# Layer normalisation's root in halves of 256 tokens, an output pair that ends one by one, and four moved or added pieces of work, in a three-layer forward pass

## The chip, the cores and the metric

One core of a Trainium2 chip runs the whole kernel. The metric is the device time in microseconds (us) of one execution; the times given are medians of three. TensorE multiplies matrices into the eight banks of PSUM (128 x 512 float32 each). VectorE, ScalarE and GpSimd (POOL in the rows) compute tile by tile, and SyncE (SP) issues the transfers that bring weights from memory. The engines run independently and wait for each other at semaphores.

## What is computed

512 tokens of width 1024, batch 1, float32. First block, two layers:

```python
for i in range(2):
    m = _even_mixer(x, ...) if i % 2 == 0 else _odd_mixer(x, ...)
    x = _layer_norm(DN_ALPHA * x + m, ln1_g[i], ln1_b[i])
    x = _layer_norm(DN_ALPHA * x + _sq_relu_mlp(x, w_up[i], w_down[i]), ln2_g[i], ln2_b[i])
    gate = jax.nn.sigmoid(x @ ple_w_gate[i] + ple_b_gate[i])
    x = x + gate * (p[i] @ ple_w_proj[i])

def _layer_norm(x, g, b):
    mu = jnp.mean(xf, -1, keepdims=True)
    var = jnp.mean(jnp.square(xf - mu), -1, keepdims=True)
    y = (xf - mu) * lax.rsqrt(var + NORM_EPS)
    return (y * g + b)
```

The even mixer joins a latent attention (queries and keys from small root-mean-square-normalised latents; each head's key is 64 own rows and a rotated part that all eight heads share) and a sliding-window attention. The odd mixer is a causal attention of 16 heads with forget gates. The hidden width of the squared-relu MLP is 4096. The second block, one layer, works on `x` after that: root-mean-square norm, four branches of 256 channels (a gated linear recurrence, pooling over time, an indexed sparse attention, attention to 256 memory vectors), a gate for each, an output projection with a norm behind it, and a gated feed-forward network of hidden width 2816.

## The kernel before

**Tiles.** Activations lie transposed: 128 channels on the partitions, 512 tokens along a row, so `X` and `ACC` have eight tiles of 128x512. Float32 products are made of three products of rounded operands: a weight tile `RAW` (up to 128x1024) is rounded to `WH` by ScalarE (`hi_ahead`, L354 to L364), and its remainder `WL` (the "low part") is made by VectorE (`lo_ahead`, `lo_one`, L366 to L380), or at some places by GpSimd (also through `lo_one`, L370), both three tiles ahead of their use, in four slots. Activations have `XH` (rounded) and `XL` (remainder). A linear output is then WH·XH, WH·XL and WL·XH over the eight tiles (L400 to L402), accumulated in one of the PSUM banks 0 and 1 in turn; an engine evacuates the bank before it is used again. Each engine's order is written out by hand, piece by piece, with the same walk over the weight tiles (`st`) on all of them.

**Layer normalisation** (four times: `ln1_0`, `ln2_0`, `ln1_1`, `ln2_1`). TensorE sums over the channels with matrices of ones (`ln_pe`, L682): the mean lies in bank 7, the mean square in bank 6. Then:
- ScalarE (`ln_act`, L745): the negative mean `MEAN`, its square, and, once VectorE has the variance, Ln and Exp (the first guess `RS` of the root) and the Square of it into bank 7 (`PB[7]`). Then the weight tile due, and the rounding of the eight tiles into `XH` (L764).
- VectorE (`ln_dve`, L788): the centred tile 0 (L791), variance (L793), floor and epsilon (L795), then one Newton step in two links (L798 in place in bank 7, L800 into bank 6), then for each tile the scale by gain and root (L806) and, one tile later, the remainder `XL` (L810). All links are 128x512.
- GpSimd (`ln_pool`, L766): the sums for mean and mean square over tiles 1 to 6 (L776, L781), then the mean added to tiles 1 to 7 of `ACC` (L783), and behind the last `XL` the sums `X = ACC + bias` of all eight tiles (L786), which the next residual uses (in the MLP, VectorE waits for all of them ahead of the first residual; in the gates, VectorE waits for tile `o` ahead of its step on output `o`).

**The pair behind each normalisation** (`lin_pair`, L1276). The first two linear outputs after it are begun together in banks 0 and 1, so that each new `XH` tile feeds four products and each `XL` tile two. Both end with the same last tile; their last two products stand directly behind each other. The third output then needs bank 0 evacuated.

**MLP** (`mlp` on each engine). Loops of four outputs: TensorE's 24 products each; VectorE makes the next low part, then the relu into `HR` (L2550), then the remainder `HL` (L2552); ScalarE rounds the weight tile three ahead, squares (L1982) and rounds (L1984). Then the down products, 16 weight tiles for 8 outputs.

**Gates of the first block** (`ple`). For each output: Tanh on ScalarE, two steps on VectorE (`GP`, then the new `X`), in layer 1 then a Square of `X` on ScalarE (L1999) that GpSimd sums up (L1143), and in between the memory vectors are transposed (L1262) and split (`ML`, L2586).

**Latent attention, keys.** VectorE rotates the shared part `KR`; GpSimd copies it below each of the eight heads' keys (`KM[64:128, h]`). VectorE writes the head's own part from each `ukv` output (L2455), behind the low part that it owes (`step()` makes the low part, then waits for the output).

**End of the recurrent branch and last gates.** GpSimd makes the low parts of nine gate weight tiles (`N_GATE[0] + 3` and on), `G_LAST[5]` among them. VectorE makes the branch's root (L712) and its output's remainder `YBL`/`y_lo` (L2961), which TensorE's gate products L1375 follow.

**Four outputs begun together** (`lin_quad`, L1549). The first four feed-forward outputs wait for the first rounded tile of the normalised input (`XH`, L2238); VectorE afterwards makes the norm's root `RU` (L3041) and the first product `TG` (L3054), which frees the first of four banks.

Of the kernel before, what the change touches and what calls it, by code (L numbers as in the profile page):

```python
# [95 lines left out]
def program(nc, known, t):  # L96
# [3 lines left out]
    with ctx:  # L100
# [358 lines left out]
        def pe_scores(pe, kind, g, qb):  # L459
# [15 lines left out]
            if kind == "mla" and qb == 0:  # L475
                evac_of(pe, M_A["uq", 2 * g])
                evac_of(pe, M_A["uq", 2 * g + 1])
                evac_of(pe, M_A["ukv", 2 * g])
                evac_of(pe, M_A["ukv", 2 * g + 1])
                pe.wait_ge(sem["chain_p"], cnt.value("chain_p", "krope"))  # L480
# [263 lines left out]

        def ln_act(act, key, b, st=None):  # L745
# [5 lines left out]
            act.wait_ge(sem["ln_v"], cnt.value("ln_v", key))  # L751
            done(act.activation(RS[:], TMP[:], ACT.Ln), "rs_ln", key)
            act.wait_ge(sem["rs_ln"], cnt.value("rs_ln", key))
            done(act.activation(RS[:], RS[:], ACT.Exp, scale=-0.5), "chain_a", ("rs", key))
            act.wait_ge(sem["chain_a"], cnt.value("chain_a", ("rs", key)))
            done(act.activation(PB[7][:], RS[:], ACT.Square), "rs_exp", key)
# [5 lines left out]
            for j in range(DT):  # L762
                act.wait_ge(sem["norm"], cnt.value("norm", (key, j)))
                done(act.activation(XH[:, j], ACC[:, j], ACT.Identity, bias=VEC[:, b + j:b + j + 1]), "x_hi", (key, j))  # L764

        def ln_pool(pool, key, b):  # L766
# [17 lines left out]
            pool.wait_ge(sem["x_lo"], cnt.value("x_lo", (key, DT - 1)))  # L784
            for j in range(DT):
                done(pool.tensor_scalar(X[:, j], ACC[:, j], VEC[:, b + j:b + j + 1], None, ALU.add), "x_full", (key, j))  # L786

        def ln_dve(dve, key, g, b):  # L788
# [4 lines left out]
            done(dve.scalar_tensor_tensor(TMP[:], PB[6][:], 1.0 / D, MEANSQ[key[:3]], ALU.mult, ALU.subtract), "chain_d", ("v", key))  # L793
            dve.wait_ge(sem["chain_d"], cnt.value("chain_d", ("v", key)))
            done(dve.tensor_scalar(TMP[:], TMP[:], 0.0, 1e-5, ALU.max, ALU.add), "ln_v", key)  # L795
            dve.wait_ge(sem["ln_v"], cnt.value("ln_v", key))
            dve.wait_ge(sem["rs_exp"], cnt.value("rs_exp", key))
            done(dve.scalar_tensor_tensor(PB[7][:], PB[7][:], -0.5, TMP[:], ALU.mult, ALU.mult), "chain_d", ("n2", key))  # L798
            dve.wait_ge(sem["chain_d"], cnt.value("chain_d", ("n2", key)))
            done(dve.scalar_tensor_tensor(PB[6][:], PB[7][:], 1.5, RS[:], ALU.add, ALU.mult), "misc_free", ("mean", key))  # L800
            dve.wait_ge(sem["misc_free"], cnt.value("misc_free", ("mean", key)))
            for j in range(DT + 1):
                if j < DT:
                    if j:
                        dve.wait_ge(sem["cen"], cnt.value("cen", (key, j)))
# [315 lines left out]
        def _(pool):  # L1121
# [7 lines left out]
            pool.wait_ge(sem["kr"], cnt.value("kr", "twice"))  # L1129
            for h in range(8):  # L1130
                x = pool.tensor_copy(KM[64:128, h], KR[64:128, :])
            done(x, "chain_p", "krope")
            pool.wait_ge(sem["chain_p"], cnt.value("chain_p", "krope"))
# [36 lines left out]
            for n in range(N_GATE[0] + 3, N_GATE[0] + 12):  # L1170
                lo_one(pool, n)
# [18 lines left out]
        def _(pe):  # L1190
# [85 lines left out]
            def lin_pair(rh, rl, names, key):  # L1276
# [7 lines left out]
                for k in range(DT + 1):  # L1284
                    if k < DT:
                        wait(pe, names[0], (key, k))
                        for e in range(2):
                            s = slots[e][0]
                            pe.matmul(PB[ms[e] % 2][:], WH[:, s, k], rh[:, k], start=k == 0, stop=False)  # L1289
                            pe.matmul(PB[ms[e] % 2][:], WL[:, s, k], rh[:, k], start=False, stop=False)  # L1290
                    if k:
                        wait(pe, names[1], (key, k - 1))
                        for e in range(2):
                            s = slots[e][0]
                            x = pe.matmul(PB[ms[e] % 2][:], WH[:, s, k - 1], rl[:, k - 1], start=False, stop=k == DT)  # L1295
                            if k == DT:
                                x.then_inc(used[s], 1)
# [3 lines left out]
            def second_pe():  # L1301
# [247 lines left out]
                def lin_quad(rh, rl, names, key):  # L1549

                    slots = [st.slot(e) for e in range(4)]
                    for o in (6, 7):
                        pe.wait_ge(sem["brf"], cnt.value("brf", o))

# [310 lines left out]
        def _(act):  # L1865
# [101 lines left out]

            def mlp(l):
                pa = st.n - 1
                for half in range(2):  # L1970
# [16 lines left out]
                    if half == 0:  # L1987
                        split_loop(16, 8)

            def ple(l):  # L1990
# [9 lines left out]
                for what in PLE_TILES:  # L2000
                    hi_ahead(act, st)
                    if isinstance(what, int):
# [4 lines left out]
                        act.activation(GT[:, what % 2], PB[b][:], ACT.Tanh, bias=HB[:, l * 8 + what:l * 8 + what + 1], scale=0.5).then_inc(evac[b], 1)  # L2007
                        st.m += 1
# [351 lines left out]
        def _(dve):  # L2360
# [55 lines left out]
            def event(what, i):  # L2416
# [778 lines left out]
```

## Time and profile before

| | us |
|---|---|
| time, median of 3 | 2248.16 (2247.05 to 2248.75) |
| the profiled execution, its own time | 2248.09 |
| its span | 2246.3 |
| TensorE busy, products | 2182.3 (97%) |
| VectorE busy | 1263.6 (56%) |
| ScalarE busy | 884.7 (39%) |
| GpSimd busy | 303.8 (14%) |

The profile is of one execution. A row of the timeline is start, duration, engine, line, operation, output and inputs with their shapes, and in brackets the idle time of the engine before it with what ended it. A row of the waits is engine, output and line of the waiting instruction, `<-` and who released it, then the total in us, the number of times and the longest. "PE" is TensorE, "DVE" VectorE, "ACT" ScalarE. Rows of an execution add up to the span, which leaves out the 1.8 us around it.

### The profile page before, as it was taken

How to read it: one execution, taken by the hardware profiler on the slowest of the kernel's cores; microseconds unless marked ns; L12 is line 12 of the kernel's file. 1: busy time of each engine (PE TensorE's matmuls, PEld its weight loads, DVE VectorE, ACT ScalarE, POOL GpSimd, SP SyncE). 2: the span in 40 equal slices, each digit the busy share in tenths (PEclk: the TensorE clock that was granted, in tenths of full speed). 3: DMA queues.
4: the chain of work that ended last, by engine and by line, in shares of the span. 5: the costliest groups of instructions: out<-in, count | busy, mean ns of one | idle time of the engine just before them, and what ended most of it. 6: DMA issues, size and time to landing. Idle time of an engine off the chain costs nothing.

```text
span 2246.3 us, 27968 instructions
## 1 busy us (share of the span) xinstructions
PE 2182.3 (97%) x10176; PEld 1725.5 (77%) x10176; DVE 1263.6 (56%) x1992; ACT 884.7 (39%) x1462; POOL 303.8 (14%) x192
## 2 busy tenths in 40 slices
PE   7999999999999999999999999999999999999998
PEld 5767788888777777788888777678778787888886
DVE  5676643343474554643343477388589678544554
ACT  3555442233254445442243254433543444222333
POOL 0000700001330001600001450133000330000001
PEclk9999999999999999999999999999999999999999
DMA  6112233333224331333333234123222232323322
GB/s 173 27 49 92 76 102 103 94 93 103 75 77 110 87 95 49 93 103 103 94 93 103 85 95 109 49 79 110 74 67 66 67 112 74 99 81 112 94 68 73
DMA packets 368307, 196.92 MB, mean 88 GB/s; under 512 B 21040, under 2 KB 362813, under 8 KB 368206
## 3 DMA queue, kind: packets, MB, share of 16 engines
q1 hardware_dynamic: 367794, 195.51, 30.4%
q8 instruction: 63, 1.03, 0.2%
q14 instruction: 38, 0.31, 0.0%
q10 hardware_dynamic: 412, 0.07, 0.0%
HBM read 193.40 MB, written 2.14 MB: 87 GB/s over the span
## 4 chain that ended last, share of the span: by engine, by line
PE 84%; DVE 9%; issue 3%; ACT 2%; POOL 1%; ACTq 0%; DVEq 0%; POOLq 0%
PE PB L400 22%; PE PB L402 21%; PE PB L401 21%; PE PB L483 2%; PE PB L529 2%; PE PB L1389 2%; PE PB L1391 2%; PE PB L1390 2%; PE PB L502 2%; DVE ATT L2925 1%; DVE WL L370 1%; POOL X L786 1%; PE PB L1289 1%; PE PB L1290 1%; PE PB L1295 1%
## 5 line engine op out<-in xcount | busy, mean ns | idle before, releaser
L364 ACT ACTIVATE WH<-RAW 128x1024 fp32r<-128x1024 f32 (+3 forms) x365 | 369.1, 1015 | 374.4 <-PE PB L402 353.4
L400 PE MATMUL PB<-XH,WH 128*128 128x512 f32 x1232 | 487.7, 396 | 6.6 <-DVE HR L2550 1.9
L402 PE MATMUL PB<-XH,WL 128*128 128x512 f32 x1232 | 480.9, 390 | 0.0
L401 PE MATMUL PB<-XL,WH 128*128 128x512 f32 x1232 | 480.0, 390 | 0.0
L380 DVE TENSOR_TENSOR WL<-RAW,WH 128x1024 fp32r<-128x1024 f32 x184 | 237.4, 1290 | 172.6 <-ACT WH L364 162.2
L400 PEld LDWEIGHTS PB<-XH,WH 128*128 128x128 f32 x1232 | 231.3, 188 | 60.7 <-issue 3.3
L402 PEld LDWEIGHTS PB<-XH,WL 128*128 128x128 f32 x1232 | 231.1, 188 | 49.5
L401 PEld LDWEIGHTS PB<-XL,WH 128*128 128x128 f32 x1232 | 231.5, 188 | 47.6 <-issue 0.7
L370 DVE TENSOR_TENSOR WL<-RAW,WH 128x1024 fp32r<-128x1024 f32 (+2 forms) x156 | 188.1, 1212 | 61.2 <-ACT WH L364 60.6
L400 PE MATMUL PB<-HH,WH 128*128 128x512 f32 x512 | 199.2, 389 | 0.0
L401 PE MATMUL PB<-HL,WH 128*128 128x512 f32 x512 | 199.2, 389 | 0.0
L402 PE MATMUL PB<-HH,WL 128*128 128x512 f32 x512 | 199.2, 389 | 0.0
L776 POOL TENSOR_TENSOR SM<-ACC 128x512 f32<-128x512 f32 x4 | 5.2, 1294 | 870.6 <-DVE ACC L2535 523.1
L1982 ACT ACTIVATE HS<-HR 128x512 f32<-128x512 f32 x64 | 40.5, 632 | 193.2 <-DVE HR L2550 193.2
L616 ACT ACTIVATE PT<-PB 128x256 f32<-128x256 f32 (+3 forms) x160 | 65.5, 412 | 124.5 <-PE PB L502 124.4
L402 PEld LDWEIGHTS PB<-HH,WL 128*128 128x128 f32 x512 | 96.1, 188 | 20.1
L400 PEld LDWEIGHTS PB<-HH,WH 128*128 128x128 f32 x512 | 96.1, 188 | 20.0
L401 PEld LDWEIGHTS PB<-HL,WH 128*128 128x128 f32 x512 | 96.1, 188 | 19.8
L2552 DVE TENSOR_TENSOR HL<-HS,HH 128x512 f32 x64 | 44.3, 692 | 107.0 <-ACT HH L1984 107.0
L370 POOL TENSOR_TENSOR WL<-RAW,WH 128x1024 fp32r<-128x1024 f32 (+1 forms) x33 | 69.0, 2103 | 260.8 <-ACT WH L364 138.4
L1389 PE MATMUL PB<-XH,WH 128*128 128x512 f32 x256 | 102.9, 402 | 0.4 <-ACT RS L2090 0.4
L1391 PE MATMUL PB<-XH,WL 128*128 128x512 f32 x256 | 99.8, 390 | 0.0
(518 smaller groups left out, 3648.3 us busy)
## 6 DMA issues: line engine op xcount, KB each, us to landing
RAW<-in_w_up SPq DMA_DIRECT2D x64, 512.0 KB, 3.9
RAW<-in_w_down SPq DMA_DIRECT2D x64, 512.0 KB, 3.6
RAW<-in_w_ffn_gate_up SPq DMA_DIRECT2D x44, 512.0 KB, 3.7
RAW<-in_w_gate SPq DMA_DIRECT2D x32, 512.0 KB, 4.0
RAW<-in_od_w_in SPq DMA_DIRECT2D x24, 512.0 KB, 6.2
RAW<-in_w_in SPq DMA_DIRECT2D x24, 512.0 KB, 4.0
RAW<-in_ple_w_gate SPq DMA_DIRECT2D x16, 512.0 KB, 3.7
RAW<-in_w_ffn_down SPq DMA_DIRECT2D x16, 512.0 KB, 4.0
```

Source lines behind the costliest of these rows:

```text
L364: act.activation(WH[:, s, 0:nb], RAW[:, s, 0:nb], ACT.Copy).then_inc(hi_done[s], 1)
L370: eng.tensor_tensor(WL[:, s, 0:nb], RAW[:, s, 0:nb], WH[:, s, 0:nb].bitcast(F32), ALU.subtract).then_inc(lo_done[s], 1)
L380: dve.tensor_tensor(WL[:, s], RAW[:, s], WH[:, s].bitcast(F32), ALU.subtract).then_inc(lo_done[s], 1)
L400: pe.matmul(PB[b][0:m, 0:n], WH[:, s, k, 0:m], rh[:, kk, :], start=kk == 0, stop=False)
L401: pe.matmul(PB[b][0:m, 0:n], WH[:, s, k, 0:m], rl[:, kk, :], start=False, stop=False)
L402: x = pe.matmul(PB[b][0:m, 0:n], WL[:, s, k, 0:m], rh[:, kk, :], start=False, stop=kk == last)
L483: xs[e] = pe.matmul(PB[2 + e][:, lo:lo + w], q[:, qb * P:qb * P + P], k[:, ks[0] * P:ks[0] * P + w], start=True, stop=plain)
L502: x = pe.transpose(PB[4 + e][:, c * P:c * P + P], PR[:, e, c * P:c * P + P], ID[:])
L529: x = pe.matmul(PB[6][e * 64:e * 64 + 64, q0 * P:q1 * P], vs[e](j), PT[:, e, j, q0 * P:q1 * P], start=first, stop=lastp)
L616: done(act.activation(PT[:, e, ks[0]:ks[0] + len(ks), qb * P:qb * P + P], PB[4 + e][:, 0:len(ks) * P].rearrange("p (j q) -> p j q", q=P), ...
L1389: pe.matmul(PB[m % 2][:], WH[:, n % 4, k], XH[:, k], start=k == 0, stop=False)
L1391: x = pe.matmul(PB[m % 2][:], WL[:, n % 4, k], XH[:, k], start=False, stop=k == DT - 1)
```

## The change

1. **Root in halves.** Variance, floor, Ln, Exp, Square, both Newton links, and scale and rounding of tile 0 are made for tokens 0 to 255 and then for 256 to 511. Variance and floor of both halves come first on VectorE; then, for each half, the Newton links and the scale. The Square no longer writes PSUM bank 7 but `VT`, a tile in SBUF, and the first Newton link works in place there. The weight tile of ScalarE stays behind both Squares.
2. **The pair ends one by one.** With the last tile the first output gets its products ahead of the second's: it ends two products ahead of it, not one.
3. **Sums by ScalarE.** The eight L786 leave GpSimd. After `ln1` ScalarE makes them between the up and the down products of the MLP's first half, after `ln2` one behind each Tanh of the gates.
4. **Key copies by ScalarE** in the slots of the first three `uq` events (3, 3, 2), and around them VectorE makes the low part after each pair of `KM` products, two at a time.
5. **Low part of `G_LAST[5]`** from GpSimd to VectorE, behind `y_lo`.
6. **Relu first** in the MLP loops: `lo_ahead` stands behind the relu, not ahead of the wait for the output.
7. **Warm products.** Ahead of the four outputs begun together TensorE makes 13 products of 512 columns whose result is overwritten.

```diff
-                pe.wait_ge(sem["chain_p"], cnt.value("chain_p", "krope"))
+                pe.wait_ge(sem["chain_a"], cnt.value("chain_a", "krope"))
...
+        TOKEN_HALVES = (slice(0, T // 2), slice(T // 2, T))
...
-            done(act.activation(RS[:], TMP[:], ACT.Ln), "rs_ln", key)
-            act.wait_ge(sem["rs_ln"], cnt.value("rs_ln", key))
-            done(act.activation(RS[:], RS[:], ACT.Exp, scale=-0.5), "chain_a", ("rs", key))
-            act.wait_ge(sem["chain_a"], cnt.value("chain_a", ("rs", key)))
-            done(act.activation(PB[7][:], RS[:], ACT.Square), "rs_exp", key)
+            for c, part in enumerate(TOKEN_HALVES):
+                act.wait_ge(sem["ln_v"], cnt.value("ln_v", (key, c)))
+                done(act.activation(RS[:, part], TMP[:, part], ACT.Ln), "rs_ln", (key, c))
+                act.wait_ge(sem["rs_ln"], cnt.value("rs_ln", (key, c)))
+                done(act.activation(RS[:, part], RS[:, part], ACT.Exp, scale=-0.5), "chain_a", ("rs", key, c))
+                act.wait_ge(sem["chain_a"], cnt.value("chain_a", ("rs", key, c)))
+                done(act.activation(VT[:, part], RS[:, part], ACT.Square), "rs_exp", (key, c))
...
-            for j in range(DT):
+            for c, part in enumerate(TOKEN_HALVES):
+                act.wait_ge(sem["norm"], cnt.value("norm", (key, "first") if c == 0 else (key, 0)))
+                x = act.activation(XH[:, 0, part], ACC[:, 0, part], ACT.Identity, bias=VEC[:, b:b + 1])
+            done(x, "x_hi", (key, 0))
+            for j in range(1, DT):
...
-            pool.wait_ge(sem["x_lo"], cnt.value("x_lo", (key, DT - 1)))
-            for j in range(DT):
-                done(pool.tensor_scalar(X[:, j], ACC[:, j], VEC[:, b + j:b + j + 1], None, ALU.add), "x_full", (key, j))
...
+            for c, part in enumerate(TOKEN_HALVES):
+                done(dve.scalar_tensor_tensor(TMP[:, part], PB[6][:, part], 1.0 / D, MEANSQ[key[:3]][:, part], ALU.mult, ALU.subtract), "chain_d", ("v", key, c))
+                dve.wait_ge(sem["chain_d"], cnt.value("chain_d", ("v", key, c)))
+                done(dve.tensor_scalar(TMP[:, part], TMP[:, part], 0.0, 1e-5, ALU.max, ALU.add), "ln_v", (key, c))
+            for c, part in enumerate(TOKEN_HALVES):
+                dve.wait_ge(sem["ln_v"], cnt.value("ln_v", (key, c)))
+                dve.wait_ge(sem["rs_exp"], cnt.value("rs_exp", (key, c)))
+                done(dve.scalar_tensor_tensor(VT[:, part], VT[:, part], -0.5, TMP[:, part], ALU.mult, ALU.mult), "chain_d", ("n2", key, c))
+                dve.wait_ge(sem["chain_d"], cnt.value("chain_d", ("n2", key, c)))
+                root = dve.scalar_tensor_tensor(PB[6][:, part], VT[:, part], 1.5, RS[:, part], ALU.add, ALU.mult)
...
+                done(dve.scalar_tensor_tensor(ACC[:, 0, part], ACC[:, 0, part], VEC[:, g:g + 1], PB[6][:, part], ALU.mult, ALU.mult), "norm", (key, "first") if c == 0 else (key, 0))
...
-            pool.wait_ge(sem["kr"], cnt.value("kr", "twice"))
-            for h in range(8):
-                x = pool.tensor_copy(KM[64:128, h], KR[64:128, :])
-            done(x, "chain_p", "krope")
-            pool.wait_ge(sem["chain_p"], cnt.value("chain_p", "krope"))
...
             for n in range(N_GATE[0] + 3, N_GATE[0] + 12):
-                lo_one(pool, n)
+                if n != G_LAST[5]:
+                    lo_one(pool, n)
...
+                wait(pe, names[0], (key, DT - 1))
+                wait(pe, names[1], (key, DT - 2))
+                rounded(0, DT - 1)
+                low(0, DT - 2)
+                rounded(1, DT - 1)
+                wait(pe, names[1], (key, DT - 1))
+                low(0, DT - 1).then_inc(used[slots[0][0]], 1)
+                low(1, DT - 2)
+                low(1, DT - 1).then_inc(used[slots[1][0]], 1)
...
+                    pe.wait_ge(lo_done[slots[0][0]], slots[0][1] + 1)
+                    for _ in range(13):
+                        pe.matmul(PB[2][:], WH[:, slots[0][0], 0], WH[:, slots[0][0], 0:4], start=True, stop=True)
...
+                    if what == "uq" and i < 3:
+                        act.wait_ge(sem["kr"], cnt.value("kr", "twice"))
+                        for h in range(3 * i, min(3 * i + 3, 8)):
+                            x = act.activation(KM[64:128, h], KR[64:128, :], ACT.Copy)
+                        if i == 2:
+                            done(x, "chain_a", "krope")
...
+            def x_full(key, j):
+                b = VCOL[key[:3] + "_b", int(key[-1])]
+                done(act.activation(X[:, j], ACC[:, j], ACT.Identity, bias=VEC[:, b + j:b + j + 1]), "x_full", (key, j))
...
                     if half == 0:
+                        for j in range(DT):
+                            x_full(f"ln1_{l}", j)
                         split_loop(16, 8)
...
+                        x_full(f"ln2_{l}", what)
...
-                    step()
+                    lin_ready(dve, st)
                     dve.tensor_tensor(KM[0:64, i], PB[b][0:64], RK[0:64, :], ALU.mult).then_inc(evac[b], 1)
+                    if i % 2:
+                        lo_one(dve, st.n + 2)
+                        lo_one(dve, st.n + 3)
...
-                            lo_ahead(dve, st, k, i, 4)
                             lin_ready(dve, st, k, i, 4)
                             b, ub = st.bank(k, i, 4)
                             dve.tensor_scalar(HR[:, k % 2], PB[b][:], 0.0, None, ALU.max).then_inc(evac[b], 1)
+                            lo_ahead(dve, st, k, i, 4)
...
+                lo_one(dve, G_LAST[5])
```

## Rows read from the trace of the kernel before

**Rows 1.** The page: the span, and the busy time of each engine.

```profile
span 2246.3 us, 27968 instructions
...
PE 2182.3 (97%) x10176; PEld 1725.5 (77%) x10176; DVE 1263.6 (56%) x1992; ACT 884.7 (39%) x1462; POOL 303.8 (14%) x192
```

**Rows 2.** Waits of TensorE by line and releaser: us in all, times, longest.

```profile
PE PB L1289 <- ACT XH L764: 8.0, 7, 1.9
...
PE PB L1262 <- DVE ML L2586: 3.9, 2, 3.5
...
PE PB L1556 <- ACT XH L2238: 3.5, 1, 3.5
...
PE PB L483 <- DVE KM L2455: 2.8, 1, 2.8
...
PE PB L400 <- DVE HR L2550: 1.9, 2, 1.4
```

**Rows 3.** Timeline of the second normalisation (start, us, engine, line).

```profile
608.07 1.05 DVE L795 TENSOR_SCALAR TMP<-TMP 128x512 f32<-128x512 f32 x1
...
608.79 1.48 POOL L783 TENSOR_TENSOR ACC<-ACC,SM 128x512 f32<-128x512 f32 x1
...
611.92 0.70 DVE L800 SCALAR_TENSOR_TENSOR PB<-PB,RS 128x512 f32<-128x512 f32 x1
...
613.96 1.28 POOL L783 TENSOR_TENSOR ACC<-ACC,SM 128x512 f32<-128x512 f32 x1
...
614.26 1.52 DVE L810 SCALAR_TENSOR_TENSOR XL<-ACC,VEC,XH 128x512 fp32r<-128x512 f32 x1 [0.20 <-ACT XH L764]
...
614.31 0.47 PE L1289 MATMUL PB<-XH,WH 128*128 128x512 f32 x1 [1.52 <-ACT XH L764]
```

**Rows 4.** Single lines: ns of one (least, median, most), from and to.

```profile
L810 DVE SCALAR_TENSOR_TENSOR XL<-ACC,VEC,XH x32: 737/740/1533, 252.7 to 1298.6; 128x512 fp32r<-128x512 f32 x32
...
L2668 DVE SCALAR_TENSOR_TENSOR MRB<-MRB,MRB x1: 425/425/425, 1346.7 to 1346.7; 128x256 f32<-128x256 f32 x1
...
L2774 DVE TENSOR_TENSOR SC<-SC,CHK x3: 294/1265/2386, 1476.8 to 1480.5; 128x128 f32<-128x128 f32 x3
```

**Rows 5.** Timeline: small additions beside GpSimd's low parts.

```profile
1476.62 2.40 POOL L370 TENSOR_TENSOR WL<-RAW,WH 128x1024 fp32r<-128x1024 f32 x1 [6.34 <-ACT WH L364]
...
1476.77 2.39 DVE L2774 TENSOR_TENSOR SC<-SC,CHK 128x128 f32<-128x128 f32 x1
...
1479.19 1.26 DVE L2774 TENSOR_TENSOR SC<-SC,CHK 128x128 f32<-128x128 f32 x1
```

**Rows 6.** Windows, TensorE: us, busy (products), granted clock, DMA share, GB/s.

```profile
350.00:400.00 50.00, 50.00 (x222) 1.00 0.32 95
...
1864.60:1867.90 3.30, 3.30 (x9) 0.50 0.46 136
```

**Rows 7.** Timeline of the gates of layer 1.

```profile
1316.33 1.55 POOL L1143 TENSOR_TENSOR SM<-SQR 128x512 f32<-128x512 f32 x1
...
1317.97 0.63 ACT L1999 ACTIVATE SQR<-X 128x512 f32<-128x512 f32 x1 [3.12 <-POOL SM L1143]
...
1320.87 0.30 PE L1262 MATMUL PB<-ID,MIN 128*128 128x128 f32 x1 [3.55 <-DVE ML L2586]
```

**Rows 8.** Timeline at the end of the recurrent branch.

```profile
1778.16 2.70 DVE L712 SCALAR_TENSOR_TENSOR HGB<-HGB,HGB 128x512 f32<-128x512 f32 x1
...
1783.06 0.47 PE L1375 MATMUL PB<-YBH,WH 128*128 128x512 f32 x1 [1.46 <-DVE YBL L2961]
```

**Rows 9.** Timeline behind the four outputs begun together.

```profile
1882.50 0.69 DVE L3041 SCALAR_TENSOR_TENSOR RU<-VT,RS 128x512 f32<-128x512 f32 x1
...
1883.29 0.69 DVE L3054 TENSOR_TENSOR TG<-PB,RU 128x512 f32<-128x512 f32 x1
...
1899.39 0.50 PE L400 MATMUL PB<-XH,WH 128*128 128x512 f32 x1 [0.56 <-DVE TG L3054]
```

**Rows 10.** Timeline before the first keys of the latent attention.

```profile
128.60 0.41 DVE L370 TENSOR_TENSOR WL<-RAW,WH 128x256 fp32r<-128x256 f32 x1
```

More of the change, by code:

```diff
@@ L750, in ln_act @@
             done(act.activation(MEANSQ[key[:3]], MEAN, ACT.Square), "m2", key)
-            act.wait_ge(sem["ln_v"], cnt.value("ln_v", key))
-            done(act.activation(RS[:], TMP[:], ACT.Ln), "rs_ln", key)
-            act.wait_ge(sem["rs_ln"], cnt.value("rs_ln", key))
-            done(act.activation(RS[:], RS[:], ACT.Exp, scale=-0.5), "chain_a", ("rs", key))
-            act.wait_ge(sem["chain_a"], cnt.value("chain_a", ("rs", key)))
-            done(act.activation(PB[7][:], RS[:], ACT.Square), "rs_exp", key)
+            for c, part in enumerate(TOKEN_HALVES):
[5 more added lines that the diff above has]
+                done(act.activation(VT[:, part], RS[:, part], ACT.Square), "rs_exp", (key, c))
             if key[:3] == "ln2":
@@ L792, in ln_dve @@
             dve.wait_ge(sem["m2"], cnt.value("m2", key))
[L793 to L798, printed above, removed]
@@ L799, in ln_dve @@
-            dve.wait_ge(sem["chain_d"], cnt.value("chain_d", ("n2", key)))
-            done(dve.scalar_tensor_tensor(PB[6][:], PB[7][:], 1.5, RS[:], ALU.add, ALU.mult), "misc_free", ("mean", key))
-            dve.wait_ge(sem["misc_free"], cnt.value("misc_free", ("mean", key)))
+            for c, part in enumerate(TOKEN_HALVES):
+                done(dve.scalar_tensor_tensor(TMP[:, part], PB[6][:, part], 1.0 / D, MEANSQ[key[:3]][:, part], ALU.mult, ALU.subtract), "chain_d", ("v", key, c))
+                dve.wait_ge(sem["chain_d"], cnt.value("chain_d", ("v", key, c)))
+                done(dve.tensor_scalar(TMP[:, part], TMP[:, part], 0.0, 1e-5, ALU.max, ALU.add), "ln_v", (key, c))
@@ new lines, in ln_dve @@
+            for c, part in enumerate(TOKEN_HALVES):
[4 more added lines that the diff above has]
+                root = dve.scalar_tensor_tensor(PB[6][:, part], VT[:, part], 1.5, RS[:, part], ALU.add, ALU.mult)
+                if c == 0:
+                    done(root, "rsq", (key, "first"))
+                    dve.wait_ge(sem["rsq"], cnt.value("rsq", (key, "first")))
+                else:
+                    done(root, "misc_free", ("mean", key))
+                    dve.wait_ge(sem["misc_free"], cnt.value("misc_free", ("mean", key)))
+                done(dve.scalar_tensor_tensor(ACC[:, 0, part], ACC[:, 0, part], VEC[:, g:g + 1], PB[6][:, part], ALU.mult, ALU.mult), "norm", (key, "first") if c == 0 else (key, 0))
@@ L802, in ln_dve @@
             for j in range(DT + 1):
-                if j < DT:
-                    if j:
-                        dve.wait_ge(sem["cen"], cnt.value("cen", (key, j)))
+                if 0 < j < DT:
+                    dve.wait_ge(sem["cen"], cnt.value("cen", (key, j)))
                     done(dve.scalar_tensor_tensor(ACC[:, j], ACC[:, j], VEC[:, g + j:g + j + 1], PB[6][:], ALU.mult, ALU.mult), "norm", (key, j))
@@ L1283, in lin_pair, with rounded, low @@
                     pe.wait_ge(lo_done[slots[e][0]], slots[e][1] + 1)
[L1284 to L1290, printed above, removed]
+                def rounded(e, k):
+                    s = slots[e][0]
+                    pe.matmul(PB[ms[e] % 2][:], WH[:, s, k], rh[:, k], start=k == 0, stop=False)
+                    pe.matmul(PB[ms[e] % 2][:], WL[:, s, k], rh[:, k], start=False, stop=False)
+                def low(e, k):
+                    return pe.matmul(PB[ms[e] % 2][:], WH[:, slots[e][0], k], rl[:, k], start=False, stop=k == DT - 1)
+                for k in range(DT - 1):
+                    wait(pe, names[0], (key, k))
+                    for e in range(2):
+                        rounded(e, k)
                     if k:
@@ L1293, in lin_pair @@
                         for e in range(2):
[L1294 to L1297, printed above, removed]
+                            low(e, k - 1)
+                wait(pe, names[0], (key, DT - 1))
[7 more added lines that the diff above has]
+                low(1, DT - 1).then_inc(used[slots[1][0]], 1)
                 st.n += 2
```

## The prediction

> **What bounds the kernel now.** I read the page first: TensorE is busy for 2182 of 2246.3 us [rows 1]. So a microsecond is won or lost only where TensorE waits, or where its products run at the lower clock. The list of TensorE's waits comes next [rows 2]. Its longest line is the one this change aims at: the first products after each of the four layer normalisations wait for the first rounded tile XH, 8.0 us in 7 waits (four of 1.5 to 1.9, three of about 0.4). The products wait once 3.5 us in the middle of the gates of layer 1, and once 3.5 us ahead of the four outputs begun together. Third, I read the second normalisation on all engines [rows 3], to see which link is late and beside what it runs. Last, the windows give the clock: in a stretch of full work 222 products take 50 us, 0.225 each; right after the 3.5 us wait the clock reads 0.50 (1.2 GHz) and 9 products take 3.3 us [rows 6]. The trace has four such falls of some 3.4 us, each costing up to 1.7 us.
>
> **The normalisation in halves.** The chain is variance, floor (L795), Ln, Exp, Square, two Newton steps (L798, L800), scale (L806), round (L764). Cutting a 128x512 link into two of 256 columns should let the two halves overlap on two engines. A half link on VectorE takes 0.43 us [rows 4]. One on ScalarE lies between 0.32 and 0.63, half and all of a full one [rows 7]; I take 0.42.
>
> But the Square no longer goes to bank 7 of PSUM. It goes to VT, in SBUF, so both Newton steps now read two SBUF tiles (VT and TMP, VT and RS), and they run while GpSimd adds the mean to seven tiles back to back (L783). The rows say what that costs. L800 reads one PSUM tile (before, its first input lies in bank 7) and one SBUF tile beside those additions and takes 0.70 [rows 3], as all eight such steps do. L810 reads two SBUF tiles: 0.74 alone, but 1.52 when it starts inside an addition [rows 3, 4], and it ends 0.55 after GpSimd's. L795 (SBUF to SBUF) is held up too, 1.05 [rows 3], against about 0.43 for the part left when GpSimd's addition ends. The closest case is two dependent additions of 128x128 behind two queued GpSimd instructions: 0.29 alone, 2.39 the first, 1.26 the second [rows 4, 5]. The second asked 0.03 us after the first had ended and still had to let GpSimd's next instruction through: 1.0 us of waiting for every such step.
>
> The Trainium skill has this as a rule (page SBUF — State Buffer, section Who interferes with whom): VectorE and GpSimd share one pair of SBUF ports, a VectorE instruction with two SBUF inputs takes it exclusively against a GpSimd one that reads SBUF, and the later one blocks until the first is through. By this rule the halves below queue up; the trace agrees (1.52 against 0.74).
>
> Worked through for the second normalisation. The first floor half ends at 608.98 (L795's end less half its work). The second floor half: 1.0 + 0.29, 610.27. First half of Newton step one: 1.0 + 0.43, 611.70 (ScalarE's three halves are over by 610.3, at worst 610.9, inside that wait). Step two 613.13, step one of the second half 614.56, step two 615.99. Scale half 0.47, round half 0.51, and the latencies of today: TensorE starts at 617.15 instead of 614.31 [rows 3], 2.8 later. All seven additions of GpSimd are used up just then. From there TensorE is fed as fast as it works (1.32 us for a tile on VectorE, six products of 0.225 on TensorE), the short wait of 0.4 goes, and L810 of tile 0 no longer stands behind GpSimd. Left: +2.4. Three times 2.4 and 1.9 for the third one, whose floor asks just as an addition ends (1.3 or 2.4): **+9.1**. Bounds from both sides: -1.3 each if no step is held up, +2.9 each if nothing is won back.
>
> The wait ahead of these products grows from 1.5 to 1.9 us to about 4.3. Waits of 3.5, 3.5 and 2.8 us [rows 2] had a fall of the clock behind them, and so had the first normalisation with 1.9; the three others, with 1.5 to 1.8, had none. At 4.3 I expect it behind all four, 1.7 us each for the three new ones: **+5.1**, bounds 0 and +7.5 (a fall of twice the length).
>
> **Outputs begun together.** Output 0 of the pair ended one product (0.225 us) ahead of output 1 and now ends two ahead, while output 1 ends as before: its evacuation starts 0.23 earlier. That counts at five places, where the third output waits for it: behind the four normalisations (0.4 to 1.4 us, two of them in [rows 2]) and behind the pair at 1822. In the third one a low part (1.2 us) stands ahead of the relu, which begins 0.6 after its bank is full; with the relu moved ahead of it that goes too. 5 x 0.23 + 0.6 = 1.75: **-1.7**, bounds 0 and -2.7. In the MLP loops the low part is still two tiles ahead of its use, so its later place costs nothing; the cover is some 9 us of products.
>
> **Sums by ScalarE.** GpSimd's eight L786 go. In the MLP, ScalarE does them (8 x 0.6 = 5 us) between the up and down products, and VectorE waits for them there; the first residual is needed two tiles, 11 us, later: nothing, with 5 us of cover left. In the gates each stands behind the Tanh: 0.6 us more before VectorE's two steps. At the end of layer 0 this uses 0.5 of 1.1 us of slack. In layer 1 the 3.5 us wait is in truth GpSimd's: it is late with its eight sums, so its first sum of squares starts at 1316.33, ScalarE's square waits for that until 1317.97, and the transposes until 1320.87 [rows 7]. With GpSimd free, that square follows the Tanh and x_full at about 1316.0. Then VectorE's X step queues behind one GpSimd addition, and the transposes come at 1319.4, of which 0.6 is already in an earlier wait. -1.5 us, and with a wait of 1.5 instead of 3.5 no fall of the clock: -1.7. Together **-3.2**, bounds +0.6 and -5.
>
> **One low part from GpSimd to VectorE.** L712 takes 2.70 us instead of 0.69 because GpSimd makes the low part of gate 5 beside it, and TensorE waits 1.46 us at its end [rows 8]. Moved behind y_lo it ends 1.5 us before its product: **-1.4**, bounds 0 and -1.5.
>
> **Key copies.** GpSimd's eight were hidden. On ScalarE the last five (2.5 us) delay a high part by 1.6 and with it VectorE by 0.3. Against that two low parts of 0.41 us, 0.33 each from start to start [rows 10], move behind the two KM products that TensorE waits for (2.8 us): **-0.4**, bounds +0.5 and -0.7.
>
> **Warm products.** 13 x 0.225 = 2.9 us fit into the 3.5 us wait ahead of the four outputs [rows 2] and keep the clock up: 1.3 us earlier for TensorE. But what is late next is VectorE. RU is finished at 1883.19 and TG starts at 1883.29 [rows 9]; from there VectorE and ScalarE run link after link until the TG that TensorE waits 0.56 us for at 1899.39. That wait grows by what was won: **-0.1**, bounds -0.1 and +1.7 (a fall of the clock behind the longer wait).
>
> **Sum.** 9.1 + 5.1 - 1.7 - 3.2 - 1.4 - 0.4 - 0.1 = +7.4. The profiled execution took 2248.09 us (span 2246.3 [rows 1]), the median is 2248.16, so they stand for each other: 2255.5 us.
>
> **Rivals.** (a) *The split works as meant.* If GpSimd lets the halves through, or they fall between its additions, each normalisation starts 1.3 us earlier and none drops the clock: -5.2 - 1.7 - 3.2 - 1.4 - 0.4 - 0.1 = -12.0, 2236 us, faster. For it: the halves are short and 0.1 us lies between two additions. Against: no two-SBUF step that starts inside a two-input GpSimd instruction gets through fast, among more than 40. It decides as soon as two of the six held steps per chain find the port free. (b) *The halves queue, but the clock holds*, or falls once: 5.1 or 3.4 less than the forecast, 2250.4 to 2252.1, no change. For it: a wait of 2.3 us at 1745 had no fall. Against: all three waits over 2.5 us had one. (c) *The falls last twice as long*, or ScalarE's added sums come late in the gates and the 3.5 us wait stays (3.2): 2259 to 2261. Against: the falls in the trace are all single.
>
> **How the numbers follow.** Forecast 0.56 (2252 to 2259, by the smaller terms' bounds; a seventh of it under +0.2%), (a) 0.17, (b) 0.17, (c) 0.10. A difference of about 0.2% (4.5 us) is what a measurement of this kernel can tell from none. Faster 0.17; same 0.17 + 0.08 = 0.25; slower 0.48 + 0.10 = 0.58. The range leaves (a) out and takes in the others with the bounds of the smaller terms (-3 at the lower end of (b), and (c) whole): 2246 to 2261.
>
> **What would show it.** Right: both halves of Newton steps one and two at 1.0 to 1.4 us instead of 0.43 beside L783; TensorE's wait for XH at 3.9 to 4.5 us, four times; windows behind it with the clock at 0.50; the transposes in the gates waiting 1 to 2 us; no wait at y_lo; a wait of about 1.8 us for TG. Wrong: Newton halves at 0.43 and a wait for XH under 1 us.

## The result and the profile after

The changed kernel takes 2259.34 us (2257.77 to 2260.14) against 2248.18; the ratio is 1.0049, 95% interval 1.0037 to 1.0061: slower by half a percent. The forecast was 2255.5, range 2246 to 2261, slower with 0.58. The profiled execution took 2257.77 us, the lowest of six, so the traces account for +9.7 us, and 1.6 us of the median stand in other executions. In all that follows one execution is left out, of the kernel with the key copies alone: it took 2444.86 us at a granted clock of 0.912.

The page of the changed kernel, its busy times (to be read against [rows 1]):

```profile
span 2255.6 us, 28037 instructions
...
PE 2187.8 (97%) x10187; PEld 1731.7 (77%) x10189; DVE 1270.4 (56%) x2013; ACT 912.3 (40%) x1518; POOL 232.6 (10%) x151
```

GpSimd has 71 us less to do, ScalarE 28 more, and neither matters: TensorE's waits do. The list of these, after (for [rows 2]: line and releaser, us in all, times, longest):

```profile
PE PB L1293 <- ACT XH L767: 17.8, 4, 4.6
...
PE PB L1269 <- DVE ML L2622: 3.3, 2, 1.7
...
PE PB L483 <- DVE KM L2488: 2.2, 1, 2.2
...
PE PB L400 <- DVE TG L3091: 1.3, 1, 1.3
...
PE PB L1576 <- ACT XH L2271: 0.6, 2, 0.3
```

The wait that the halves should shorten went from 8.0 us in seven waits to 17.8 in four. Those at ML, KM and ahead of the four outputs are shorter, the one at TG longer. Why XH is late stands in the timeline of the second normalisation (for [rows 3]; start, us, engine, line, operation, tiles, and in brackets the idle time before with its releaser; x7 are seven instructions joined):

```profile
606.17 9.38 POOL L790 TENSOR_TENSOR ACC<-ACC,SM 128x512 f32<-128x512 f32 x7 [9.17 <-ACT SM L750]
...
607.67 1.18 DVE L800 TENSOR_SCALAR TMP<-TMP 128x256 f32<-128x256 f32 x1
...
609.22 0.94 DVE L800 TENSOR_SCALAR TMP<-TMP 128x256 f32<-128x256 f32 x1
...
610.32 1.28 DVE L804 SCALAR_TENSOR_TENSOR VT<-VT,TMP 128x256 f32<-128x256 f32 x1
...
611.63 1.41 DVE L806 SCALAR_TENSOR_TENSOR PB<-VT,RS 128x256 f32<-128x256 f32 x1
613.08 0.48 DVE L813 SCALAR_TENSOR_TENSOR ACC<-ACC,VEC,PB 128x256 f32<-128x256 f32 x1
613.47 0.96 DVE L804 SCALAR_TENSOR_TENSOR VT<-VT,TMP 128x256 f32<-128x256 f32 x1
...
614.47 1.37 DVE L806 SCALAR_TENSOR_TENSOR PB<-VT,RS 128x256 f32<-128x256 f32 x1
...
617.05 0.77 PE L1293 MATMUL PB<-XH,WH 128*128 128x512 f32 x1 [4.39 <-ACT XH L767]
```

Six links of 256 columns take 0.94 to 1.41 us, while L813, as wide but with a PSUM input, takes 0.48 among them. A link that was 0.70 at full width [rows 3] takes 1.41 at half. The windows of TensorE (us, busy with products in brackets, granted clock, DMA share, GB/s) show what followed the wait, for [rows 6]:

```profile
350.00:400.00 50.00, 50.00 (x223) 1.00 0.36 105
617.00:621.50 4.50, 4.45 (x11) 0.50 0.02 5
...
615.50:622.20 6.70, 5.15 (x12) 0.50 0.01 4
622.40:626.00 3.60, 3.60 (x18) 1.00 0.00 0
253.70:257.00 3.30, 3.30 (x9) 0.50 0.00 0
...
1755.60:1757.40 1.80, 1.77 (x8) 0.50 0.00 0
```

In the second normalisation the clock is at 0.50 from 615.5 on, while TensorE still waits, and until 622.3, 6.8 us in all. Twelve products in it take 5.15 us, against 2.7 at 0.225 each: 2.4 us are lost, at three of the four normalisations. The first has a fall of 3.4 us, as it had before.

Laid side by side, product by product, the two timelines give where the changed kernel falls behind (+) or catches up, worked out from the start of the same product in both (us; the rows add up to +9.4, which is, but for rounding, what the two spans differ by):

| stretch | forecast | measured |
|---|---|---|
| key copies and the clock behind KM | -0.4 | -2.5 |
| start behind the four normalisations | +2.8, +2.8, +2.3, +2.8 | +2.5, +2.9, +2.9, +2.9 |
| from there to the third output: slow products, short waits gone, the pair, the relu | +2.0 | +3.6 |
| gates of layer 1 | -3.2 | -2.5 |
| fall of the clock behind the 2.3 us wait in the recurrent branch | 0 | +1.6 |
| low part of gate 5 | -1.4 | -1.6 |
| pair at 1822, warm products up to TG | -0.3 | -0.4 |

### The profile page after: what moved, and what is told of

It is laid out like the page before. It is cut to its first block, busy times and chain, and to the rows that moved or that the text cites. A ratio compares the mean times of both kernels' runs of the same rounds, so it can differ in the third digit from the quotient of the medians.

```text
span 2255.6 us, 28037 instructions
## 1 busy us (share of the span) xinstructions
PE 2187.8 (97%) x10187; PEld 1731.7 (77%) x10189; DVE 1270.4 (56%) x2013; ACT 912.3 (40%) x1518; POOL 232.6 (10%) x151
## 4 chain that ended last, share of the span: by engine, by line
PE 85%; DVE 9%; issue 3%; ACT 2%; DMA 0%; POOL 0%; DVEq 0%; SPq 0%; ACTq 0%; POOLq 0%
PE PB L400 21%; PE PB L402 21%; PE PB L401 21%; PE PB L483 2%; PE PB L1406 2%; PE PB L1408 2%; PE PB L1407 2%; PE PB L529 2%; PE PB L502 2%; PE PB L1293 1%; PE PB L1294 1%; DVE ATT L2961 1%; PE PB L1297 1%; DVE WL L370 1%; DVE PB L806 0%
## 5 line engine op out<-in xcount | busy, mean ns | idle before, releaser
L401 PE MATMUL PB<-XL,WH 128*128 128x512 f32 x1232 | 479.5, 389 | 0.0
L2585 DVE TENSOR_SCALAR HR<-PB 128x512 f32<-128x512 f32 x64 | 44.3, 692 | 147.9 <-PE PB L402 143.7
L1407 PE MATMUL PB<-XL,WH 128*128 128x512 f32 x256 | 99.7, 390 | 0.0
```

The source lines that it names most:

```text
L401: pe.matmul(PB[b][0:m, 0:n], WH[:, s, k, 0:m], rl[:, kk, :], start=False, stop=False)
L1407: pe.matmul(PB[m % 2][:], WH[:, n % 4, k], XL[:, k], start=False, stop=False)
```

## Experiments

**Where the loss sits.** Two kernels divide the change. In one the normalisation's functions on ScalarE and VectorE are the old ones, all else is changed:

```diff
-            for c, part in enumerate(TOKEN_HALVES):
-                act.wait_ge(sem["ln_v"], cnt.value("ln_v", (key, c)))
...
-                done(act.activation(VT[:, part], RS[:, part], ACT.Square), "rs_exp", (key, c))
...
+            done(act.activation(RS[:], TMP[:], ACT.Ln), "rs_ln", key)
...
+            done(act.activation(PB[7][:], RS[:], ACT.Square), "rs_exp", key)
```

> The changed kernel with the normalisation as before: full width, Square in bank 7; the sums X + bias stay on ScalarE, and the other parts of the change stay. The traces put +11.1 us of later starts and +4.6 us of slower products behind them on the halves; without them 2259.3 - 15 = 2244 us, 4 under the kernel before, 1.6 either way with the fall of the clock behind the wait of 2.3 us in the recurrent branch. If the other parts cost as much as they bring, 2248.

2240.79 us, ratio 0.997 (0.9957 to 0.9982): faster than before. The other has the halves alone, on the kernel before.

> The kernel before with the normalisation's halves alone, GpSimd's sums X + bias still behind them. If the halves carry the loss, 2248.2 + 15 = 2263 us, or a little more since the pair's and the relu's gains are missing: slower than the whole change. If the loss needs another part of the change too, under 2259.

2263.67 us, ratio 1.0065 (1.0048 to 1.0081). So the halves cost 15.3 us alone, by the runs of the kernel before made beside it (2248.35), and 18.5 within the change. Everything else together brings 7.6 us without them and 4.3 with them. The first kernel came out 3 us under what was expected; its trace has neither the fall of the clock behind the first normalisation (wait 1.87 us) nor that in the recurrent branch (2.25 us). It has one at a place where no other trace has it, behind two idle times of 0.7 us:

```profile
680.80:684.10 3.30, 3.30 (x13) 0.50 0.02 7
```

Its six executions, at 2239.5 to 2243.7, have granted clocks of 0.998 down to 0.995. That fits a fall behind a wait near 2 us in some executions and not in others, but only one of the six has a trace.

**Width or place of the operands.** Full width again, but the Square still in VT (the conditions that ask for the first part follow and are left out here):

```diff
-        TOKEN_HALVES = (slice(0, T // 2), slice(T // 2, T))
+        TOKEN_HALVES = (slice(0, T),)
```

> The changed kernel with the root at full width again (one part of 512 tokens), but the Square still in VT, so that both Newton links still have two inputs in SBUF. The old normalisation at full width, with bank 7, gave 2240.8 us. If the place of the operands costs and not the width, two links per normalisation are held by GpSimd (0.6 to 0.7 us over their 0.69 each), TensorE's wait for XH is 2.3 to 3 us, and the slow products behind it stay: about 2249 us. If VT is harmless, 2241.

2248.86 us, ratio 1.0005 (0.9996 to 1.0014), 8 us over the same width with bank 7, and a wait of 3.0 us on average. Its waits, and its second Newton link (ns: least, median, most):

```profile
PE PB L1293 <- ACT XH L767: 12.1, 4, 3.9
```

```profile
L806 DVE SCALAR_TENSOR_TENSOR PB<-VT,RS x4: 1641/1655/1660, 250.6 to 1290.5; 128x512 f32<-128x512 f32 x4
```

1.65 us where the same step with a PSUM input took 0.70 [rows 3]. The place of the Square alone is worth 8 of the 18.5 us. The other 10.5 come with the halving, which makes twice as many links, each of them held.

The smallest undoing: the first Newton link writes bank 7, so that only the second link has a PSUM input.

```diff
-                done(dve.scalar_tensor_tensor(VT[:, part], VT[:, part], -0.5, TMP[:, part], ...
+                done(dve.scalar_tensor_tensor(PB[7][:, part], VT[:, part], -0.5, TMP[:, part], ...
-                root = dve.scalar_tensor_tensor(PB[6][:, part], VT[:, part], 1.5, RS[:, part], ...
+                root = dve.scalar_tensor_tensor(PB[6][:, part], PB[7][:, part], 1.5, RS[:, part], ...
```

> The changed kernel, where each half's first Newton link reads VT and TMP as before but writes PSUM bank 7, so that the second reads PSUM and one SBUF tile. By the port: the two root halves (L806, 1.37 to 1.41 us) fall to 0.43, the two first Newton halves stay at 0.9 to 1.3; TensorE's wait for XH falls from 4.4 to 2.3 to 2.9 us; 1.5 to 2.1 us four times, with the falls of the clock still there: about 2252 us. If halving costs by itself, nothing changes: 2258 to 2260.

2245.29 us, ratio 0.9987 (0.9978 to 0.9997), 14 us gone with one operand (11 between the two profiled executions). More than expected: TensorE's wait came to 2.05 us (second normalisation), the falls behind it are 8 products instead of 12, and the first Newton link of the second half asked at a better moment (0.53 us instead of 0.96). The second link in the changed kernel, and then both links here:

```profile
L806 DVE SCALAR_TENSOR_TENSOR PB<-VT,RS x8: 1373/1388/1414, 247.3 to 1297.1; 128x256 f32<-128x256 f32 x8
```

```profile
L804 DVE SCALAR_TENSOR_TENSOR PB<-VT,TMP x8: 533/918/1295, 248.2 to 1288.5; 128x256 f32<-128x256 f32 x8
L806 DVE SCALAR_TENSOR_TENSOR PB<-PB,RS x8: 432/432/433, 249.5 to 1289.1; 128x256 f32<-128x256 f32 x8
```

The first link writes PSUM here and is held all the same, up to 1.30 us: what counts is where a link reads.

**Is GpSimd the holder?** Same VectorE code as in the change, but GpSimd's additions begin only when the root is done:

```diff
+            pool.wait_ge(sem["misc_free"], cnt.value("misc_free", ("mean", key)))
             for j in range(1, DT):
                 done(pool.tensor_tensor(ACC[:, j], ACC[:, j], MEAN, ALU.add), "cen", (key, j))
```

> The changed kernel; GpSimd's seven additions (mean to tiles 1 to 7) wait until the second root half is done, all else stays. By the port: both floor and both Newton halves take 0.43 us, TensorE's first wait for XH falls below 0.8 us; but then the tiles are fed by GpSimd at 1.3 us or more, with L821 beside it, so that new waits of 0.2 to 1 us stand between the tiles: 2243 to 2259 us, likeliest 2250. If halving costs by itself, the first wait stays above 3 us and the time goes above 2265.

2244.34 us, ratio 0.9985 (0.9975 to 0.9994). The links that the change made slow, unchanged in form:

```profile
L801 DVE TENSOR_SCALAR TMP<-TMP x8: 293/294/295, 243.6 to 1281.0; 128x256 f32<-128x256 f32 x8
...
L805 DVE SCALAR_TENSOR_TENSOR VT<-VT,TMP x8: 417/422/426, 245.4 to 1283.4; 128x256 f32<-128x256 f32 x8
L807 DVE SCALAR_TENSOR_TENSOR PB<-VT,RS x8: 432/433/434, 245.8 to 1283.8; 128x256 f32<-128x256 f32 x8
...
610.42 0.47 PE L1294 MATMUL PB<-XH,WH 128*128 128x512 f32 x1 [0.23 <-ACT XH L767]
```

This settles it: only the time of another engine's work changed. The floor halves, 0.93 to 1.43 us in the changed kernel, take 0.29, and the Newton halves, 0.97 to 1.41 there, take 0.42 to 0.43. The halves by themselves do what they were made for: TensorE waits 0.23 us where the kernel before waits 1.52, the 1.3 us of rival (a). What is given back stands behind it: the tiles come in GpSimd's time, and TensorE waits 0.60 us for the second one.

**Halves with a PSUM input in every link.** Variance and floor at full width in place in bank 6, ScalarE's Ln reads bank 6 (both halves first, then Exp and Square of each, left out here), the Newton links go through bank 7:

```diff
+            done(dve.scalar_tensor_tensor(PB[6][:], PB[6][:], 1.0 / D, MEANSQ[key[:3]], ALU.mult, ALU.subtract), "chain_d", ("v", key))
...
+            done(dve.tensor_scalar(PB[6][:], PB[6][:], 0.0, 1e-5, ALU.max, ALU.add), "ln_v", key)
...
+                done(dve.scalar_tensor_tensor(PB[7][:, part], VT[:, part], -0.5, PB[6][:, part], ALU.mult, ALU.mult), "chain_d", ("n2", key, c))
...
+                root = dve.scalar_tensor_tensor(PB[6][:, part], PB[7][:, part], 1.5, RS[:, part], ALU.add, ALU.mult)
```

> The changed kernel with halves from Ln on, but no link with all its inputs in SBUF: variance and floor at full width in place in bank 6, ScalarE's Ln reads bank 6 (both halves first, then Exp and Square of each into VT), the first Newton link reads VT and bank 6 and writes bank 7, the second reads bank 7. By the port: every half link 0.43 us and every full one 0.69 beside GpSimd's additions; TensorE's wait for XH 0.7 to 1.1 us, no fall of the clock behind it: 3.4 us four times and three or four falls of 1.9: about 2240 us, as with the old normalisation or a little under. If halving costs by itself: above 2250.

2238.27 us, ratio 0.9953 (0.9936 to 0.9969), the lowest median with all of the change's other parts, 2.5 us under the old normalisation (the two intervals overlap). The link

```profile
L804 DVE SCALAR_TENSOR_TENSOR VT<-VT,TMP x8: 965/1118/1284, 246.0 to 1296.1; 128x256 f32<-128x256 f32 x8
```

is the changed kernel's first Newton half. In this one, with its wait:

```profile
L804 DVE SCALAR_TENSOR_TENSOR PB<-VT,PB x8: 420/427/430, 247.9 to 1281.4; 128x256 f32<-128x256 f32 x8
...
611.30 1.92 DVE L821 SCALAR_TENSOR_TENSOR XL<-ACC,VEC,XH 128x512 fp32r<-128x512 f32 x1
611.34 0.47 PE L1293 MATMUL PB<-XH,WH 128*128 128x512 f32 x1 [0.96 <-ACT XH L768]
```

All eight first Newton halves take 0.43 beside GpSimd's additions. The next step with two SBUF inputs, the remainder of tile 0, is held instead: 1.92 us. A second execution of the same kernel was profiled by itself.

> A second look at the halves without links that lie in SBUF alone, as they are: 2238.3 us, with the waits as in its first trace.

It took 2239.3 us. Two kernels that keep the Square itself in bank 7 in halves were written and have no time: in them ScalarE would write the bank's second half while VectorE works in its first, and nothing orders the two, so they never ran.

**What the slow products come from.** 17 overwritten products in the wait of the changed kernel:

```diff
+                if key[:2] == "ln":
+                    for _ in range(17):
+                        pe.matmul(PB[ms[0] % 2][:], WH[:, slots[0][0], 0], WH[:, slots[0][0], 0:4], start=True, stop=True)
```

> The changed kernel with 17 products of 512 columns (3.8 us at 0.225) ahead of the pair behind each normalisation, in the wait of 4.4 us; they are overwritten. Nothing starts earlier. If the slow products behind the wait come from TensorE's idleness, the four stretches at 0.50 behind the normalisations go, 1.6 to 2.2 us each: about 2252 us. If they come from something else (the load that sets in), 2259.

2249.4 us, ratio 1.0004 (0.9994 to 1.0013): 10 us less with nothing starting earlier. In its windows the clock reads 1.00 where the change had 0.50:

```profile
615.00:619.00 4.00, 3.50 (x16) 1.00 0.00 0
619.00:623.00 4.00, 4.00 (x19) 1.00 0.01 2
```

Product by product its trace catches up 1.6 us behind the first normalisation and 2.4 behind each of the other three, 8.8 in all, which is what the four falls cost. It has none in the recurrent branch either (1.6 us), where it waits 2.3 us as the changed kernel does, but one at KM (1.8) that the changed kernel's trace lacks.

**The small parts by themselves**, each on the kernel before. Key copies and the low parts behind KM (the lines that leave GpSimd are left out here):

```diff
+                    if what == "uq" and i < 3:
...
+                            x = act.activation(KM[64:128, h], KR[64:128, :], ACT.Copy)
...
+                    if i % 2:
+                        lo_one(dve, st.n + 2)
+                        lo_one(dve, st.n + 3)
```

> The kernel before with the key copies on ScalarE and the low parts after the KM products, nothing else. My forecast gave this -0.4 us (2247.8), with the fall of the clock behind TensorE's wait for KM kept. The trace of the whole change shows 0.7 us less of that wait (2.17 instead of 2.84) and no slow products behind it, 1.5 us: if both come from this part, 2246.0 us; if the fall went by chance or through another part, 2247.5.

2246.35 us, ratio 0.9995 (0.9986 to 1.0004): the interval takes in no change; in the profiled execution the gain is 0.7 of the wait and 1.6 of the clock. Seven executions lie at 2245.9 to 2246.8 us and three at 2247.8 to 2248.0, about as far apart as a fall costs. The first line is the products' wait for KM, the second the window behind it:

```profile
129.77 0.35 PE L483 MATMUL PB<-KM,QM 128*128 128x128 f32 x1 [2.18 <-DVE KM L2456]
...
130.40:133.80 3.40, 3.40 (x23) 1.00 0.48 96
```

The kernel before, behind its wait of 2.8 us:

```profile
131.00:134.40 3.40, 3.40 (x12) 0.56 0.12 35
```

The sums X + bias on ScalarE:

```diff
-            pool.wait_ge(sem["x_lo"], cnt.value("x_lo", (key, DT - 1)))
-            for j in range(DT):
-                done(pool.tensor_scalar(X[:, j], ...), "x_full", (key, j))
...
+                        for j in range(DT):
+                            x_full(f"ln1_{l}", j)
...
+                        x_full(f"ln2_{l}", what)
```

> The kernel before with the sums X + bias on ScalarE, nothing else. Forecast -3.2 us, 2245.0. The trace of the whole change shows 2.1 us in the gates of layer 1 (1.28 later at the first transposes, 1.88 earlier at the second, 1.5 for slow products that are gone): 2246 us. If ScalarE's eight sums in the MLP delay something, more than 2247.5.

2247.13 us, ratio 0.9996 (0.9987 to 1.0005), again not to be told from no change by the time alone. In the trace the gates bring 2.2 us (2.5 in the whole change), and 1.2 are lost later, where the fall behind the 3.5 us wait lasts 6.8 us in this execution instead of 3.4. Nothing in the MLP is delayed.

The halves with PSUM inputs without the 13 warm products (`range(0)` for `range(13)`):

> The halves without links in SBUF alone (2238.3 us), without the 13 warm products. Forecast: TensorE starts the four outputs at the same time, its first products run at 0.50 and cost it some 1.4 us, and all of that comes out of its wait for TG, 1.28 us with them and near 0 to 0.6 without: 2238.3 to 2238.6 us. If the warm products are worth what they save TensorE, 2239.7.

2239.01 us, ratio 0.9963 (0.9949 to 0.9976), against 0.9953 with them: no difference that these runs can tell. Its waits, without and (second fence) with the warm products:

```profile
PE PB L1576 <- ACT XH L2271: 3.5, 1, 3.5
...
PE PB L400 <- DVE TG L3091: 0.6, 1, 0.6
```

```profile
PE PB L400 <- DVE TG L3091: 1.3, 1, 1.3
PE PB L1576 <- ACT XH L2271: 0.6, 2, 0.3
```

What TensorE saves in front it waits at TG. Last, an attempt at the 2.3 us wait of the recurrent branch, on the same base: three of nine pieces of gate products ahead of it.

```diff
+                level_fill(3)
                 pe.wait_ge(sem["hg_x"], cnt.value("hg_x", (7, 1)))
...
-                level_fill(9)
+                level_fill(6)
```

> The halves without links in SBUF alone, and in the recurrent branch three of the nine pieces of gate products behind the level-7 products moved ahead of TensorE's wait of 2.3 us: 2.0 us of work that is due anyway fills the wait. If nothing behind runs short of cover, 2 us less and no fall of the clock there: about 2236.3 us. If the six pieces left no longer cover the next wait, or the moved pieces wait for GpSimd's low parts, 2238 to 2240.

2238.88 us, ratio 0.9958 (0.9945 to 0.9972): nothing won. Of the wait 0.22 us are left, and 4 us behind its products there is a new one:

```profile
1746.12 0.48 PE L1510 MATMUL PB<-XX 128*128 128x256 f32 x1 [1.72 <-DVE XX L2953]
```

Without the move the same products start at 1745.99 us, with it at 1746.12: VectorE's chain of copies and products sets the end there, not TensorE's order.

## Why the prediction was right, and where it was off

**The held links: right in kind and size.** The step "1.0 us of waiting for every such step", taken from two additions of 128x128 [rows 4, 5], forecast 1.43 for a Newton half and TensorE at 617.15 in the second normalisation. The trace has 0.96 to 1.41 and 617.05. That GpSimd holds these links, and by the place of their inputs, was argued then. The kernel whose GpSimd work begins later shows the first, the kernels that move operands the second. The rule of the Trainium skill (page SBUF — State Buffer, section Who interferes with whom) also says that a VectorE instruction with at most one SBUF input does not contend, unless it runs in one of the modes that use two ports; eight of eight links at 0.43 beside GpSimd's additions agree. The floor halves have one SBUF input too and were held; that they run in such a mode is argued, not shown. It says too that the later of two blocks until the first is through: GpSimd's seven additions took 9.38 us here and 8.78 with the PSUM links, so both sides pay.

**The normalisations' sum, +9.1, too low by about 0.5.** The third was taken as 1.9, since its floor would ask just as an addition ends; it started 2.85 later, like the others.

**The clock, +5.1, too low by about 2.** That it falls behind three more normalisations was right; the term was mis-sized, 2.4 us each instead of 1.7. The stretches at 0.50 last 6.8 us, twice the 3.4 of the four in the trace before; this is what rival (c) says, and the bound of +7.5 was meant for it, against 7.2 here. They cost less than double since they begin while TensorE still waits. The kernel with 17 products in the wait shows that the idleness is their cause. In the table this is +3.6 against +2.0, since about 0.5 more than forecast was won back there. Not forecast at all was the fall in the recurrent branch, +1.6: I had taken "a wait of 2.3 us had no fall" as a fixed property of that wait. Thirteen of the fourteen traces have this wait, at 2.25 to 2.30 us: three show a fall behind it (the changed kernel, the one at full width with VT, the one with late additions), ten do not. What decides it is open.

**The pair and the relu, -1.7: right.** Behind the third normalisation the wait of 1.4 us became 0.3, behind the others 0.55 became 0.33; 0.2 at 1822.

**The gates, -3.2, against -2.5.** The wait of 3.55 us became two of 1.65 and 1.67 (it was forecast as one of 1.5), since the first transposes come 1.3 later; the fall of the clock went, as forecast.

**Low part of gate 5, -1.4: right** (-1.6). L712 takes 0.69 again and the wait is gone.

**Key copies, -0.4, against -2.5.** The mechanism was right (0.7 of the wait, forecast 0.4), and the failed step is the clock: the fall behind the wait was kept in the sum. I took waits over 2.5 us as those with a fall, and did not ask on which side 2.84 less something would come out. It came out at 2.17 without one. That is half luck: of the eleven traces with these key copies, with waits of 2.16 to 2.35 us, six have a fall there. So the part is worth 0.7 us in each and some 1.6 more in about every second one.

**Warm products, -0.1: right** by the kernel without them, and in kind by the wait at TG, which took back what was won in front; it grew to 1.28 us, not to the 1.8 that was forecast.

The sum was +7.4, the profiled execution has +9.7. By the table the terms missed by +4.4 us and by -2.4, the larger part of the second through the fall at KM that did not come, so that the sum is nearer than its terms is in part luck. The median, 2259.34, lies just above the 2252 to 2259 of the forecast itself and in the band of rival (c), whose longer falls came while its other half, a 3.5 us wait left in the gates, did not. The other 1.6 us of the median are in no trace: the granted clock reads 0.992 in the profiled execution and 0.991 in the other five, which is the size of one more fall, but where it is I can't say.

## What to carry to other kernels

Before a VectorE chain is cut finer or its tiles are moved, look at what GpSimd does meanwhile: a link with all its inputs in SBUF pays, in this kernel, for one GpSimd instruction each time it asks, so halves double the price, while one input in PSUM makes it free (1.39 to 0.43 us, 14 of 2259 us for one operand). A scratch tile in PSUM that seems arbitrary may be what keeps a chain fast. And price what follows TensorE's waits, in both directions: shortening one from 2.8 to 2.2 us brought 0.7 and, in some executions, 1.6 behind it; lengthening one from 1.5 to 4.4 cost 2.9 and 2.4.

## What the runs showed of the hardware

- A fall of the clock behind a wait of TensorE is no fixed function of the wait. In the fourteen traces, leaving out their first and last 20 us, no wait of 1.65 to 1.8 us has one behind it. Between 1.86 and 2.7 us the same wait at the same place has it in one trace and not in the next (1.86 to 1.89 us at the first normalisation: 3 of 4; 2.25 to 2.30 us in the recurrent branch: 3 of 13; 2.16 to 2.35 at KM: 6 of 11; 2.65 with and 2.67 without in one trace). All twenty of 2.8 to 4.6 us have it. One fall, at 680.8 us in the kernel with the old normalisation, has no wait over 0.8 us in the 9 us ahead of it.
- The stretch at 0.50 has one of two lengths in these traces, about 3.4 or 6.8 us, and the wait does not fix which: behind the same wait of 3.46 to 3.47 us ahead of the four outputs it was 3.4 us in two traces (9 and 8 slow products) and 6.8 in three (13 or 14). The long ones stood only behind waits of 2.9 us and more.
- The executions of one kernel differ by their granted clock: with the old normalisation, 2239.5 us at 0.998, 2242.8 at 0.996, 2243.7 at 0.995. That single falls make the difference is likely by their cost (1.6 to 2.4 us), but a single trace does not show it.
- A VectorE instruction that asks just before GpSimd's running one ends can be held through the next one too: L821, 0.75 us alone, took 1.92. It asked at 611.30, about 0.1 us before the sixth addition ended, and ended at 613.22, 0.55 behind the seventh.
